# Reordering the first twelve microseconds of a two-layer kernel: norm columns in their own transfer, input quarters turned between the products

## The reference

```python
def rms_norm(x, g):
    x32 = x.astype(jnp.float32)
    y = x32 * lax.rsqrt(jnp.mean(x32 * x32, axis=-1, keepdims=True) + EPS)
    return (y * g.astype(jnp.float32)).astype(x.dtype)

h = rms_norm(x, norm_g)                      # x: (1, 256, 2048)
proj = jnp.einsum('bsd,dn->bsn', h, w_in)    # then split into 13 parts, q_a first
```

## Time and profile before

| | |
|---|---|
| median of 3 runs | 2106.39 us |
| lowest, highest | 2105.9, 2107.35 us |
| the profiled execution, its own time | 2106.43 us |
| its span | 2104.2 us |
| time outside the span | 2.23 us |
| TensorE busy | 2085.2 us |
| VectorE, ScalarE, GpSimd busy | 1442.1, 1084.4, 39.6 us |
| DMA over the span | 402.60 MB, mean 191 GB/s |

### The profile page before, as it was taken

One profiled execution on the slowest core, in us unless ns is written; L12 is line 12 of the kernel. 1 busy time (PEld: TensorE's weight loads), 2 busy tenths in 40 slices (PEclk: granted clock), 3 DMA queues, 4 the chain that ended last, 5 costly groups with the idle time before them and its releaser, 6 DMA issues.

```text
span 2104.2 us, 24976 instructions
## 1 busy us (share of the span) xinstructions
PE 2085.2 (99%) x10059; PEld 1751.8 (83%) x10059; DVE 1442.1 (69%) x1872; ACT 1084.4 (52%) x1412; POOL 39.6 (2%) x49
## 2 busy tenths in 40 slices
PE   8999999999999999999999999999999999999998
PEld 6888888888888888888888888888888888888886
DVE  5977788875555786556554455466896796796684
ACT  5455555555444675554454454354544554454453
POOL 0000000000000020000000000000000000000000
PEclk9999999999999999999999999999999999999999
DMA  7555555564565544365755542455555465456562
GB/s 273 180 196 188 196 200 202 188 244 185 180 224 197 182 158 160 140 221 199 296 184 187 188 160 101 162 198 190 195 207 189 169 232 183 178 199 220 183 220 98
DMA packets 56803, 402.60 MB, mean 191 GB/s; under 512 B 6256, under 2 KB 6640, under 8 KB 9584
## 3 DMA queue, kind: packets, MB, share of 16 engines
q1 hardware_dynamic: 53648, 380.61, 50.3%
q0 software_dynamic: 2608, 19.66, 2.4%
q10 hardware_dynamic: 432, 0.73, 0.1%
HBM read 392.59 MB, written 8.39 MB: 191 GB/s over the span
## 4 chain that ended last, share of the span: by engine, by line
PE 96%; DVE 1%; ACT 1%; issue 1%; DMA 0%; SPq 0%; POOLq 0%; POOL 0%; DVEq 0%; ACTq 0%
PE proj L619 15%; PE proj L621 15%; PE proj L620 15%; PE proj L1092 11%; PE proj L1096 6%; PE proj L732 4%; PE proj L734 4%; PE proj L733 4%; PE tbank L732 2%; PE tbank L733 2%; PE tbank L734 2%; PE tbank L578 2%; PE bank_a L732 1%; PE bank_a L734 1%; PE bank_a L733 1%; PE bank_b L732 1%
## 5 line engine op out<-in xcount | busy, mean ns | idle before, releaser
L1747 DVE TENSOR_TENSOR w_lo<-raw,w_hi 128x1024 fp32r<-128x1024 f32 x630 | 747.1, 1200 | 517.0 <-ACT w_hi L1203 509.5
L1203 ACT ACTIVATE w_hi<-raw 128x1024 fp32r<-128x1024 f32 x630 | 647.9, 1040 | 745.7 <-PE proj L621 466.2
L619 PE MATMUL proj<-w_hi,a_both 128*128 128x512 f32 x1280 | 512.6, 401 | 0.0
L621 PE MATMUL proj<-w_hi,a_both 128*128 128x512 f32 x1280 | 500.3, 391 | 0.0
L620 PE MATMUL proj<-w_lo,a_both 128*128 128x512 f32 x1280 | 499.0, 390 | 0.0
L621 PEld LDWEIGHTS proj<-w_hi,a_both 128*128 128x128 f32 x1280 | 240.5, 188 | 51.8
L620 PEld LDWEIGHTS proj<-w_lo,a_both 128*128 128x128 f32 x1280 | 241.0, 188 | 47.5
L619 PEld LDWEIGHTS proj<-w_hi,a_both 128*128 128x128 f32 x1280 | 241.0, 188 | 47.0
L1092 PE MATMUL proj<-a_both,w_hi 128*128 128x512 f32 x672 | 160.6, 391 | 0.3 <-DVE a_both L1793 0.3
L1092 PEld LDWEIGHTS proj<-a_both,w_hi 128*128 128x128 f32 x672 | 123.5, 188 | 24.5 <-DVE a_both L1793 0.5
L1203 ACT ACTIVATE w_hi_deep<-raw 128x1024 fp32r<-128x1024 f32 x84 | 83.6, 1021 | 95.1 <-PE proj L1096 59.5
(11 more groups left out here) (524 smaller groups left out, 2999.3 us busy)
## 6 DMA issues: line engine op xcount, KB each, us to landing
raw<-stream SPq DMA_DIRECT2D x358, 1024.0 KB, 4.8
nat<-x SPq DMA_DIRECT2D x4, 512.0 KB, 9.6
z_store<-z POOLq DMA_DIRECT2D x1, 2048.0 KB, 8.4
ga_store<-z POOLq DMA_DIRECT2D x1, 2048.0 KB, 12.1
gb_store<-z POOLq DMA_DIRECT2D x4, 512.0 KB, 7.2
yb<-z_store POOLq DMA_DIRECT2D x4, 512.0 KB, 9.6
ga<-ga_store POOLq DMA_DIRECT2D x1, 2048.0 KB, 8.1
gb<-gb_store POOLq DMA_DIRECT2D x1, 2048.0 KB, 14.3
```

The source lines that it names most:

```text
L619: nc.tensor.matmul(banks[t][:, :], ah, wh, start=first, stop=False)
L621: last = nc.tensor.matmul(banks[t][:, :], al, wh, start=False, stop=end)
L1203: A(hi_places[s][:, 0:width], src, ACT.Copy).then_inc(w_rounded, 1)
L1747: V.tensor_tensor(lo_places[s][:, 0:width], src, hi_places[s][:, 0:width].bitcast(f32), SUB).then_inc(w_rest, 1)
```

## The change

It does five things. The 16 columns of `norm_g` get a transfer and a semaphore of their own, issued first on ACT's queue, ahead of the identity; the other 266 columns of `par` follow behind the identity. ACT and DVE wait for `norm_g_ready` ahead of group 0, and for `par_ready` only behind group 7. TensorE no longer turns quarter 1 ahead of piece 0: it turns quarters 1, 2 and 3 behind pieces 0, 2 and 4. ACT and DVE do pieces 0 to 2 behind groups 0 and 1, pieces 3 to 5 behind groups 2 and 3, pieces 6 and 7 behind groups 4 and 5, and none behind groups 6 and 7. ACT's two square sums now follow one another, ahead of pieces 8 to 11.

```diff
+        norm_g_ready = sem("norm_g_ready")
@@ TensorE
             turn_x(0)
-            turn_x(1)
             readers += [by_dve] * 8
             by_dve.add(8)
             tr.add(8)
 
             def first_slot(j):
-                if j in (0, 2):
-                    turn_x(j // 2 + 2)
+                if j in (0, 2, 4):
+                    turn_x(j // 2 + 1)
@@ ScalarE
+            norm_g = PARAMS["norm_g"]
+            act.dma_start(par[:, norm_g], params_in[:, norm_g]).then_inc(norm_g_ready, 16)
             act.dma_start(cst[:, CONSTS["ident"]], consts_in[:, CONSTS["ident"]]).then_inc(ident_ready, 16)
-            act.dma_start(par[:, :], params_in).then_inc(par_ready, 16)
+            act.dma_start(par[:, norm_g.stop:], params_in[:, norm_g.stop:]).then_inc(par_ready, 16)
             act.wait_ge(pool_init, 1)
             A(e_warm, neg_half[:, 0:1], ACT.Copy)
-            act.wait_ge(par_ready, 16)
-            for c, n in enumerate((2, 2, 1, 2)):
+            act.wait_ge(norm_g_ready, 16)
+            for c, n in enumerate((3, 3, 2, 0)):
                 for g in (2 * c, 2 * c + 1):
                     high(a_hi, 2 * g, "norm_g", 2 * g, x_banks)
                 split(n)
+            act.wait_ge(par_ready, 16)
             square_sum(scr[:, :], nat[:, 0, :], ss1[:, 0:1])
-            split()
             square_sum(scr[:, :], nat[:, 1, :], ss1[:, 1:2])
             split(RING)
@@ VectorE
-            dve.wait_ge(par_ready, 16)
-            for c, n in enumerate((2, 2, 1, 2)):
+            dve.wait_ge(norm_g_ready, 16)
+            for c, n in enumerate((3, 3, 2, 0)):
                 for g in (2 * c, 2 * c + 1):
                     low(a_hi, a_lo, 2 * g, "norm_g", 2 * g, x_banks)
                 split(n)
-            split()
+            dve.wait_ge(par_ready, 16)
             dve.wait_ge(sumsq, 2)
             mean(ms1[:, :], ss1[:, :], D)
             split(RING)
```

## The result

| | before | after |
|---|---|---|
| median | 2106.76 us (20 runs) | 2109.52 us (20 runs) |
| lowest, highest | 2105.9, 2107.46 us | 2108.66, 2110.46 us |
| ratio, 95% interval | | 1.0014, 1.0008 to 1.002 |
| the profiled execution | 2106.43 us | 2110.13 us |
| its span | 2104.2 us | 2107.9 us |

The changed kernel is slower by 2.76 us, 0.14%, clear of the interval. The forecast was +0.06 us, nothing, and the stated range ended at 2108.0 us.

What follows compares the result with a forecast made beforehand. TensorE bounds the kernel, idle mainly in the head. First product at 10.6 us, piece 0 4.73 us and the rest 21.79 us put chunk 1 at 37.12 against 37.06 us: +0.06 us, 2106.4 us; range 2104.9 to 2108.0 us.

Steps and rivals of the forecast that it cites:

- What bounds the kernel: Whole span: TensorE is 96% of the last-ending chain; the change touches one head wait, prize at most 3.54 us.
- the identity's landing: Head, ACT's queue: identity now second, issued 0.48 us later, lands at about 4.92 us, no cost.
- Rival 2: Head, ACT's queue: small load delays the identity or arrives late itself; +2.7 us, 2109.1 us; chance 0.09.
- The norm columns: Head, first on ACT's queue: the 8 KB load taken to need 3.7 us, as the identity did in that place.
- The next limit: Head: weights' first half, landing at 8.03 us, is late next; first product at 10.6 us, a wait of 3.5 us remains.
- The pace: Piece 0 on TensorE: ten products at 0.427 us, two at 0.23 us, 4.73 us; rise 4.25 us after TensorE resumes.
- Rival 1: Piece 0 on TensorE: the clock rises with the products, 2.63 us after the first; -0.65 us, 2105.7 us; chance 0.22.
- The upper bound of +1.6 us: Piece 0 and the turn behind it: late rise, piece 0 takes 5.12 us and the turn 1.97 us, +0.45 and +1.17.
- What had to hide: Up to chunk 1: later turns, `par_ready` and piece 8 behind the squares cost nothing; piece 8 tightest, 0.65 us spare.

Runs made afterwards that it cites:

- one-transfer kernel: Changed kernel with the norm columns put behind the identity so one transfer brings both, whole `par` second; 2107.32 us, +0.76 us against before.
- par-later kernel: One-transfer kernel with `par` issued on ACT only behind groups 0 and 1 and three roundings; 2106.81 us, +0.09 us against before.
- identity later: Kernel before with the identity still first on ACT's queue but issued at 2.11 us, behind SP's first weights; 2109.46 us, one run.
- loads alone: Kernel before with only the transfers changed, turns and pieces in the old order; 2107.74 us, +1.18 us against before.
- piece first: Par-later kernel with ACT and DVE doing weight piece 0 between groups 0 and 1; 2105.57 us, -1.15 us against before.
- 16 packets ahead: Changed kernel with a 16-packet transfer replacing the norm columns first on ACT's queue, whole `par` third, both engines waiting for it; 2110.29 us, one run.
- weights held: Changed kernel, but SP issues the first weights only once the identity has landed; 2107.81 us, one run.
- gap-filled kernel: Kernel before with seven unused products of 128 columns between TensorE's first two turns; 2105.39 us, -1.57 us against before.

## Why the prediction was wrong

**What bounds the kernel: right.** Only the head moved; from 19.82 us to chunk 1 TensorE's rows after have no wait, and the difference at 40.81 us is the difference of the spans.

**The failed step: the identity's landing.** The prediction said "it lands at about 4.92 us, just before x: no cost", from 3.7 us of flight and an issue 0.48 us later. It landed at 8.2 us. The flight of a row was carried over to another moment of issue. The row that spoke against it was there: `par`, issued at 1.22 us, took 7.0 us. I put that down to its 141 KB ("Against: `par` is large"); the runs show 8 KB at 6.5 us in that company, and 133 KB at 3.8 us without it. Rival 2 had the mechanism and its sum right: first turn at 8.3 us, first product at 13.3 us, +2.7 us, 2109.1 us; measured 8.22 us, 13.41 us, +2.76 us, 2109.52 us. That the total agrees within 0.1 us is in part luck: the profiled pair differs by 3.7 us, and the rival's sum has no term for the pace. What failed there is its chance, 0.09, and with it the range, which ended at 2108.0 us. Which part of SP's stream holds the small loads up, and how, stays open.

**The norm columns: right.** 3.7 us, as taken. The rule of the Trainium skill, "DMA: Bandwidth & Descriptors", section "Rules for kernel authors", to join small transfers into a large one, would have been the better guide: joined, the kernel was 2.0 us quicker than the changed one. But the price is not that of small transfers as such, since 8 KB in the first place were as quick as 64; it is that of the one behind them, which is issued 0.48 us later.

**The next limit: right.** In the one-transfer kernel the identity is as early as the forecast had it. There the wait for the weights' first half, its rounding and its rest takes the place of the wait for x (3.97 us), and the first product comes at 11.07 us against 10.6. That one wait would be replaced by another as long was the reason to forecast nothing, and it holds: +0.76 us. The par-later kernel meets the numbers (10.67 us, +0.09 us), but ACT's groups set them there, so that this agreement is in part luck.

**The pace: mis-sized in the profiled execution.** "I take +0.06 us, since TensorE resumes at the same moment behind the same idle stretch" presumed ten slow products. The changed kernel had twelve and a slow part of the turn, +0.88 us together; the one-transfer kernel twelve too (piece 0 from 11.07 to 16.32 us, 5.25 us). The medians leave no room for most of this, as said above. Rival 1 wanted the rise 2.6 us behind the first product, as before (14.81 - 12.18). In none of the other kernels without added products did it come so soon: with a turn right ahead 3.1 us (identity later) and 3.8 us (loads alone), without one 3.4 us (piece first) to more than 5.2 us (changed kernel). The upper bound of +1.6 us held, but one term in it was misread: 1.97 us is the duration of the slow turn with its modelled end, while the 0.80 us of the quick turn is the distance to the next start. By starts the slow turn takes 1.62 us ahead of the first product (10.56 to 12.18) and 1.77 us ahead of another turn (9.80 to 11.57 in the run with the identity later), so the bound should have been near +1.4 us. The sum of the forecast does not use it, but the upper end of the range does.

**What had to hide, did.** Quarters 1 to 3 (no wait of TensorE ahead of pieces 2, 4, 6), `par_ready`, and the tightest one, piece 8 behind both square sums: TensorE's rows after show no wait up to chunk 1's start at 40.81 us.

## What to carry to other kernels

In the first microseconds of this kernel, what counted for a small load that everything waits for was whether it was issued before the stream of weights on another queue, and not its size (8 to 141 KB) or its place in its own queue. So join what is needed first into one transfer, issue it first, and issue later what nobody needs yet (`par`: 1.4 us on the landing of the weights). A duration read from the trace belongs to its company; where a neighbour in time took twice as long, both ends go into the range with more than a token chance. Work that TensorE does during a wait is not free to move behind it: here the wait hid a whole turn. And a wait of TensorE can be worth filling even with products that nobody reads: by the medians it took 1.57 us off the kernel before, and 3.02 us, clear of the interval, together with the piece-first order.

## What the runs showed of the hardware

- Three transfers of 8, 64 and 133 KB on ACT's queue landed 3.8 to 3.9 us after issue with 512 KB of x beside them, and 3.7, 7.0 and 8.2 us with the weights' 512 KB transfers issued from 1.23 us on; 1 KB on GpSimd's queue took 4.1 and 7.1 us. Which part of the way holds them isn't settled. In the run with the identity later, ACT's queue moved no packet until 6.5 us, though the identity had been issued at 2.11 us, and then 105 up to 8.5 us. In the run with 16 packets ahead it moved 25 from 2.5 to 4.5 us and 103 from 4.5 to 6.5 us, against 286 from 2.5 to 4.5 us with the weights held. So in the first of these most of the added delay lies before the packets move; in the second they also move slowly once begun. No run separates the making of descriptors from the reading.
- With seven fp32 products of 128 columns (14 rows in the trace) in TensorE's wait, the turn behind them already ran at the quick pace; with eight products of zeros ahead of the first turn, that turn did nearly so (5.13 to 6.27 us, 1.14 us, against 1.74 us in the gap-filled kernel, 4.90 to 6.64). An idle stretch of 2.19 us ahead of the first product didn't bring the slow pace back there.
- The run-to-run spread was 1.6 us before and 0.35 us once TensorE was busy from 1.3 us on. That it is mostly the moment of the rise is likely, but none of the outlying runs has a profile. Whether transposes count for the rise as products do stays open: right behind a turn it came 2.6 us (before), 3.1 us (identity later) and 3.8 us (loads alone) behind the first product, and 3.4 to over 5.2 us where none stood ahead, one execution each. No run here bears out or refutes the Trainium skill, "TensorE: Matmul & The Clock Gate", section "Part 4: PE-mode transpose", on that.
